# Layer 0's expert results: gathered and summed in a stage of their own, or inside layer 1's first projection sweep

## The reference

```
proj = modulate(rms_norm(x)) @ w_in          # queries, keys, values of three attention branches
x    = x + mod[2] * merge_branches(...)      # this is "x1" in the kernel
h2   = modulate(rms_norm(x))
f    = hier_moe(h2)                          # top-2 of 32 SwiGLU experts: f = w0 * ye[row0] + w1 * ye[row1]
x    = x + mod[5] * f                        # "x2", the input of the next layer
```

## Time and profile before

| | us |
|---|---|
| median of 3 runs | 5008.48 |
| the profiled execution's own time | 5003.68 |
| its span | 5002.1 |
| PE busy | 4544.4 (91%) |
| DVE busy | 3310.6 (66%) |
| ACT busy | 2464.5 (49%) |
| POOL busy | 1192.3 (24%) |
| layer 0's jobs, about | 1927 to 2584 |
| layer 0's combine and change of stage, about | 2584 to 2637 |
| layer 1's jobs, about | 4244 to 4957 |
| layer 1's combine, about | 4957 to 5002 |

### The profile page before, as it was taken

The page is one execution under the profiler, slowest core; times in us unless marked ns, Lnnn a source line. Parts: engine busy times, 40 slices in busy tenths (PEclk is TensorE's granted clock), DMA queues, the critical chain, the costliest instruction groups (busy, mean ns, idle before and its releaser), DMA issues. The chain is left out here.

```text
span 5002.1 us, 75983 instructions
## 1 busy us (share of the span) xinstructions
PE 4544.4 (91%) x25973; PEld 3776.1 (75%) x25973; DVE 3310.6 (66%) x5272; ACT 2464.5 (49%) x3056; POOL 1192.3 (24%) x921
## 2 busy tenths in 40 slices
PE   6999998889999897999967999999999987999995
PEld 4887877777877875877745878888877866788774
DVE  6653667676776567777777626677756436877776
ACT  3223555564233315777743225655633222777774
POOL 3650004400000013333334620043000001333333
PEclk8999999999999998999988999999999998999998
DMA  5645234264554566999995635253556345999998
GB/s 188 206 120 122 65 87 104 100 185 139 209 201 168 207 210 262 397 397 397 397 357 169 199 113 117 63 124 97 136 191 217 113 167 174 388 397 397 397 397 330
DMA packets 581798, 1088.92 MB, mean 218 GB/s; under 512 B 111876, under 2 KB 265380, under 8 KB 578552
## 3 DMA queue, kind: packets, MB, share of 16 engines
q1 hardware_dynamic: 531952, 919.40, 54.8%
q0 software_dynamic: 36272, 119.42, 6.6%
q10 hardware_dynamic: 13400, 47.85, 2.4%
HBM read 903.12 MB, written 183.43 MB: 217 GB/s over the span
## 5 line engine op out<-in xcount | busy, mean ns | idle before, releaser
L1800 PE MATMUL merge_acc<-ahead_wide,merge_w_split 128*128 128x512 f32 (+1 forms) x2880 | 638.7, 377 | 20.5 <-DMA ahead_wide<-hT 14.9
L1800 PEld LDWEIGHTS merge_acc<-ahead_wide,merge_w_split 128*128 128x128 f32 x2880 | 505.4, 190 | 128.6 <-issue 18.7
L648 PE MATMUL project_proj_acc<-ahead_wide,project_hT 128*128 128x512 f32 x2280 | 562.1, 399 | 3.0 <-DVE ahead_wide L471 1.7
L2502 DVE TENSOR_TENSOR experts_w_gate<-experts_raw_gate,experts_w_gate 128x2048 fp32r<-128x2048 f32 x146 | 363.4, 2495 | 295.8 <-ACT experts_w_gate L2398 295.8
L648 PEld LDWEIGHTS project_proj_acc<-ahead_wide,project_hT 128*128 128x128 f32 x2280 | 426.1, 191 | 94.0 <-DVE project_hT L501 4.6
L2377 POOL TENSOR_TENSOR experts_w_down<-experts_raw_down,experts_w_down 128x2048 fp32r<-128x2048 f32 x73 | 355.9, 4876 | 512.5 <-ACT experts_w_down L2398 512.5
L2549 PE MATMUL experts_gate_acc<-experts_w_gate,experts_rowsT 128*128 128x512 f32 x1752 | 432.2, 403 | 13.2 <-DVE experts_rowsT L2507 6.9
L964 DVE TENSOR_REDUCE attend_stat<-attend_scores 128x1 f32<-128x1280 f32 (+2 forms) x288 | 305.7, 1061 | 205.9 <-PE attend_scores L865 202.2
L2563 PE MATMUL experts_result_acc<-experts_w_down,experts_hiddenT 128*128 128x512 f32 x1752 | 430.1, 401 | 12.2 <-DVE experts_w_down L2502 12.2
L2549 PE MATMUL experts_up_acc<-experts_w_up,experts_rowsT 128*128 128x512 f32 x1752 | 420.6, 395 | 0.0
L2549 PEld LDWEIGHTS experts_gate_acc<-experts_w_gate,experts_rowsT 128*128 128x128 f32 x1752 | 327.0, 190 | 101.5 <-issue 22.0
(11 more groups left out here) (257 smaller groups left out, 8298.5 us busy)
## 6 DMA issues: line engine op xcount, KB each, us to landing
experts_raw_gate<-in_w_exp_gate_dram SPq DMA_DIRECT2D x146, 1024.0 KB, 13.8
experts_raw_up<-in_w_exp_up_dram SPq DMA_DIRECT2D x146, 1024.0 KB, 12.8
experts_raw_down<-in_w_exp_down_dram SPq DMA_DIRECT2D x146, 1024.0 KB, 11.4
ahead_rows<-in_w_merge_dram SPq DMA_DIRECT2D x120, 768.0 KB, 6.4
merge_mod_w_ada<-in_w_ada_rows_dram POOLq DMA_DIRECT2D x80, 512.0 KB, 3.7
qk<-project_staged SPq DMA_DIRECT2D x74, 512.0 KB, 3.4
ye<-ahead_rows ACTq DMA_DIRECT2D x73, 512.0 KB, 6.3
attend_keys<-qk SPq DMA_DIRECT2D x96, 320.0 KB, 5.6
```

The lines of the kernel that those rows point to most:

```text
L648: m = pe.matmul(acc[g % 2][:, :], hT[:, a, q * KP + k, t * P:(t + 1) * P], w_split[n % SLOTS][:, c, k, :], start=(q == 0 and i == 0 and k ...
L1800: m = pe.matmul(acc[:, b, 0:w], w_split[b][:, a, k, :], hT[:, x, k, 0:w], start=(i == 0 and k == 0), stop=(i == 2 and k == KD - 1))
L2502: dve.tensor_tensor(w[n][:, 1, half, :], raw[n][:, half, :], w[n][:, 0, half, :].bitcast(F32), ALU.subtract).then_inc(w_lo[n].sem, 1)
```

## The change

1. In layer 0 there is no combine. The rows and weights that it used (`row_of`, `weight`) move into two small buffers that live through the whole kernel (`carried`), and the experts' stage returns after the jobs.
2. In both layers the job's result is multiplied by the gate row on its way out of PSUM. VectorE does it (`result`), after the lo of down's first half; ScalarE's copy is gone, and ScalarE only issues the store, for the job before. Where there are context tokens (layer 0), VectorE first picks the gate row per token: a compare on the token's number (GpSimd copies the numbers to `row_token`), a `scalar_tensor_tensor` of two gate rows into `y`, and then the product. The gate rows (1 MB) are loaded at the start of the jobs.
3. In layer 1's projection GpSimd gathers the two rows of each tile, two buffers each, which lie in split buffers that sweep 1's weights use later. VectorE adds both to the `x1` tile in place, with two `scalar_tensor_tensor` (`add_results`), ScalarE stores the latent tiles to `x2` (`store_x2`), and the norm's in-place scaling waits for that store. The splits of sweep 1's first two pieces move from steps 3 and 5 to 7 and 8.
4. Layer 1's combine has two `scalar_tensor_tensor` on VectorE per tile in place of ScalarE's product and VectorE's three operations.

```diff
 def project_heads(nc, io, scr, l, nq, st, inner, ident, hT, ahead, carried):
+    SUM = l > 0
+    result = [[w_split[4 + b][:, c, :, :].rearrange("p k n -> p (k n)").bitcast(F32) for b in range(2)] for c in range(2)]
+    split_at = (7, 8) if SUM else (3, 5)
...
 # SyncE
+                src = scr["x1"][t * P:(t + 1) * P, :] if SUM else stream_rows(io, scr, l, t)
+                sp.dma_start(xh[t % RING][:, :], src).then_inc(x_in[t % RING].sem, 16)
...
 # ScalarE
+            def store_x2(t):
+                act.wait_ge(x_ready.sem, x_ready.done(t))
+                act.dma_start(scr["x2"][t * P:(t + 1) * P, :], xh[t % RING][:, :]).then_inc(x2_out[t % 2].sem, 16)
...
+            if SUM:
+                store_x2(0)
             norm(0)
+            if SUM:
+                store_x2(1)
             norm(1)
...
                     if 0 <= g - 2 < n_heads:
                         heads_hi(g - 2)
+                    if SUM and p == 0 and s + 3 < NL:
+                        store_x2(s + 3)
...
 # VectorE
+            def add_results(t):
+                x, b = xh[t % RING], t % 2
+                dve.wait_ge(x_in[t % RING].sem, x_in[t % RING].done(t // RING))
+                dve.wait_ge(result_in[0][b].sem, result_in[0][b].done(t // 2))
+                dve.scalar_tensor_tensor(out=x[:, :], in0=result[0][b], scalar=carried.weight[:, 0, t:t + 1],
+                                         in1=x[:, :], op0=ALU.mult, op1=ALU.add).then_inc(added.sem, 1)
+                dve.wait_ge(result_in[1][b].sem, result_in[1][b].done(t // 2))
+                dve.wait_ge(added.sem, added.done(t))
+                dve.scalar_tensor_tensor(out=x[:, :], in0=result[1][b], scalar=carried.weight[:, 1, t:t + 1],
+                                         in1=x[:, :], op0=ALU.mult, op1=ALU.add).then_inc(x_ready.sem, 1)
...
                 dve.wait_ge(nrs.sem, nrs.done(t))
+                if SUM and t < NL:
+                    dve.wait_ge(x2_out[t % 2].sem, x2_out[t % 2].done(t // 2))
                 dve.scalar_tensor_tensor(out=x[:, :], in0=x[:, :], scalar=n_stat[:, b, 3:4],
...
                         if s + 1 < NT:
                             norm_lo(s + 1)
+                        if SUM and s + 3 < NT:
+                            add_results(s + 3)
...
 # GpSimd: gather(0), gather(1) first; gather(2), gather(3) after the first table; then ahead of each rotation
+                    if SUM and p == 0 and s + 4 < NT:
+                        gather(s + 4)
                     rotate(first[p] + s)
 
 def run_experts(...):
 # SyncE, after the first job's down weights
+            mod_rows(scr, l, 5, gate[:, :, :], sp).then_inc(gate_in.sem, 16)
...
 # ScalarE
-            def result(g):
-                act.wait_ge(dm.sem, dm.done(g))
-                if later(g, 1):
-                    act.wait_ge(y_out.sem, y_out.done(g - 1))
-                act.copy(y, acc_y[:, :]).then_inc(yd.sem, 1)
+            def store_result(g):
                 act.wait_ge(yd.sem, yd.done(g))
                 act.dma_start(scr["ye"][ds(g * P, P), :], y).then_inc(y_out.sem, 16)
...
-                if later(g, 1):
-                    result(g - 1)
+                if later(g, 2):
+                    store_result(g - 2)
                 act.wait_ge(ht.sem, ht.done(g))
...
 # VectorE
+            def result(g):
+                dve.wait_ge(dm.sem, dm.done(g))
+                if later(g, 1):
+                    dve.wait_ge(y_out.sem, y_out.done(g - 1))
+                row_gate = gate[:, 0, :]
+                if CONTEXT:
+                    dve.wait_ge(kind_read.sem, kind_read.done(g))
+                    take_waits(dve, gate_taken)
+                    dve.tensor_scalar(of_context[:, :], row_token[:, ds(g, 1)], float(NL * P), None, ALU.is_ge
+                                      ).then_inc(kind_known.sem, 1)
+                    dve.wait_ge(kind_known.sem, kind_known.done(g))
+                    dve.scalar_tensor_tensor(out=y, in0=gate[:, 1, :], scalar=of_context[:, 0:1],
+                                             in1=gate[:, 0, :], op0=ALU.mult, op1=ALU.add).then_inc(gate_picked.sem, 1)
+                    dve.wait_ge(gate_picked.sem, gate_picked.done(g))
+                    row_gate = y
+                dve.tensor_tensor(y, acc_y[:, :], row_gate, ALU.mult).then_inc(yd.sem, 1)
...
                 split(DOWN, g)
+                if later(g, 1):
+                    result(g - 1)
...
             result_rows()
             weights()
+            result(n_jobs - 1)
```

More of the change, by code:

```diff
@@ L261, in project_heads @@
     taken = st.event("pool_waits_taken")
+    added, x_ready = st.event("first_result_added"), st.event("x2_ready")
+    x2_out = [st.dma(f"x2_stored{b}") for b in range(2)]
+    result_in = [[st.pool_dma(f"result{c}_gathered{b}") for b in range(2)] for c in range(2)] if SUM else None
+    split_at = (7, 8) if SUM else (3, 5)
     tr, hh, hl, v_ev = (st.event("head_transposed"), st.event("head_hi"), st.event("head_lo"),
@@ L585, in rotate, with gather @@
                                    ).then_inc(tn.sem, 1)
+            def gather(t):
+                if t >= 2:
+                    pool.wait_ge(x_ready.sem, x_ready.done(t - 2))
+                take_waits(pool, taken)
+                for c in range(2):
+                    pool.indirect_dma_start(
+                        out=result[c][t % 2], out_offset=None, in_=scr["ye"],
+                        in_offset=bass.IndirectOffsetOnAxis(ap=carried.row_of[:, t, c:c + 1].bitcast(U32), axis=0)
+                    ).then_inc(result_in[c][t % 2].sem, 16)
             TABLE_AT = {(0, 3): 1, (0, 5): 2, (1, 2): 3, (2, 2): 4, (3, 2): 5}
+            if SUM:
+                gather(0)
+                gather(1)
             pool.wait_ge(tab_in.sem, tab_in.done(1))
@@ L2590, in _, with combine @@
             down(n_jobs - 1)
-def combine(nc, io, scr, l, nq, st, inner, row_of, weight, gate, gate_in, x1, x1_in, out):
+def combine(nc, io, scr, l, nq, st, inner, row_of, weight, x1, x1_in, out):
     y = [[st.sb(f"y{c}_{t}", [P, D], F32, inner) for t in range(nq)] for c in range(2)]
```

97 lines of the change are left out of this document (61 added, 36 removed).

## The result

The changed kernel takes 5074.82 us (median of 4 runs, 5069.22 to 5078.06), the kernel before 5007.78 beside it (5005.16 to 5009.58): ratio 1.0134, 95% interval 1.0122 to 1.0146, 1.3% slower. The forecast was 5074. The profiled execution took 5078.06 with a span of 5076.4, so 74.3 us are to be found between the two spans. That is 7 us more than the 67.0 between the two medians: this execution is the slowest of its four, and the profiled one of the kernel before (5003.68) is faster than any of its runs.

What follows compares the result with a forecast made beforehand. It took TensorE (99% busy, DMA also full) to bound the jobs, and DMA and VectorE the combine. 60 + 10 - 48 + 15 + 20 + 12 - 3.5 = +65.5 us gave 5069.2 profiled, 5074 median, range 5050 to 5098.

Steps and rivals of the forecast that it cites:

- a: Layer 0's jobs: period grows from 18.4 to 20.3 us as VectorE's down split is held beside GpSimd, +60 us.
- GpSimd lost only 0.9 us: Layer 0's jobs: GpSimd's down split, started beside VectorE's, took 5.72 instead of 4.80 us, so was barely held.
- the long state: Layer 0's jobs: the lost tie repeats itself, holding the period at 20.3 us for 32 of 34 periods.
- b: Last job of layer 0, from last gate product to last store issued: +10 us, bounds 5 and 13.
- c: Layer 0's combine goes, between last store issued and layer 1's first load: -48 us, bounds 46 and 49.
- d: Start of layer 1's projection: first transposes 9 us later, tile 2 adds 6, together +15 us, bounds 6 and 22.
- e: Sweep 0 of layer 1's projection, paced by VectorE, with result additions and waits for x2's store: +20 us, bounds 14 and 32.
- all of it visible: Sweep 0: seven steps' additions of 2 x 1.3 us on VectorE, 18.2 us, lengthen the sweep in full.
- f: Layer 1's jobs: the result's product can make VectorE's down split lose to GpSimd, +12 us, bounds 0 and 25.
- the first jobs run back to back and lose the race: Layer 1's first jobs: GpSimd starts before VectorE's down split; the reason for taking 12 of a possible 14 us.
- g: Layer 1's tail: VectorE's four steps per tile become two, transfers limit the gain, -3.5 us, bounds -8 and 0.
- the transfers' 30 us: Layer 1's tail: 16 gathers and 8 stores, 12.6 MB at 420 GB/s, need 30 of the 36.5 us.

Runs made afterwards that it cites:

- vector_all: Changed kernel, but VectorE splits both halves of the down weights in layer 0's jobs and GpSimd none: 5007.96 us, ratio 1.0010.
- no_pick: Changed kernel without the compare and scalar_tensor_tensor that choose layer 0's gate row, so context rows get a wrong gate: 5002.65 us, ratio 0.9999.
- reordered: Changed kernel with VectorE's gate-row choice behind the next gate split, its product ahead of the down split, and ScalarE's store behind the silu: 5028.11 us, ratio 1.0054.
- pool_copy: Changed kernel with GpSimd's tensor_tensor for the down weights replaced by a one-input tensor_copy, values wrong: 5000.63 us, ratio 0.9992.
- gate_late: Changed kernel with the 1 MB of gate rows loaded behind the first job's gate and up weights instead of ahead: 5068.34 us, ratio 1.0129.
- short_add: Changed kernel, but from tile 3 on the second result is added to only 128 of 1024 columns in layer 1's first sweep: 5063.18 us, ratio 1.0125.

## Why the prediction was right, and where it was off

**a, right (59.3 for 60).** The period is 20.21 for 20.3, from the fourth on (31 of 34; the first three are 19.4, 19.4 and 18.6). The marks came out: the down split held (6.38 us in the mean), the scalar_tensor_tensor short because it comes after GpSimd, TensorE released by VectorE's result. vector_all, no_pick and the periods of reordered show that the hold is the cause. **One step in it was wrong**: "GpSimd lost only 0.9 us". The 4.80 I compared with was itself held. In the kernel before GpSimd's instruction starts beside the end of VectorE's down split; in the early job of the earlier trace rows that split is:

```profile
1949.78 2.29 DVE L2502 TENSOR_TENSOR experts_w_down<-experts_raw_down,experts_w_down 128x2048 fp32r<-128x2048 f32 x1
```

With 1.24 us of it left (1952.07 - 1950.83) GpSimd took 5.72; with 0.33 left, 4.80 to 4.83 in most jobs; with 1.50 left, 5.99. All are 4.5 and what was left: each engine is held for all that remains of the other's instruction. (In no_pick, where in most jobs the split was already over, GpSimd takes 4.60 to 4.63.) The Trainium skill, page "SBUF — State Buffer", section "SBUF: two separate sides", says just this of the port pair that VectorE and GpSimd share: it is an exclusive lock, and the one who comes second blocks fully. The rows now agree for both sides. The page counts a VectorE instruction with two SBUF inputs only against a GpSimd instruction that reads SBUF; pool_copy agrees that one such input is enough on GpSimd's side. The slip made no difference to the sum, since in the long state GpSimd always comes first, and the two periods of reordered in which it came last are 20.3 as well.

**b, right (11.6 for 10)**; the choice of the gate row was held 4 us in the last job as well (5.33), and no_pick gave it back. The 1.6 over the forecast are mostly in the product of the job before: it took 7.41 us behind TensorE's wait, where the forecast has about 6.

**c, right (48.1 for 48).** The combine's stage is gone with all but one landing and the change of stage.

**d and e, right as a sum, with the parts off.** They are +10.1 for 9 to the first transposes, then +29.8 for 26, and +26.7 to +29.8 over the six kernels with that code. Of the 29.8, 12.6 lie between tile 0's and tile 2's transposes (9.4 to 12.6 over the six), where the forecast has 6, and 17.1 behind them, where it has 20. What the sum left out at the start is the last of the four weight pieces: SP issues its load 7.9 us after the first transposes, before it was 4.1, and ScalarE can cast it 15.9 us after them instead of 8.0 (11.0 in vector_all, 11.8 in gate_late). Tile 2's additions are queued behind its split. The cast before and after:

```profile
2657.05 1.05 ACT L403 CAST ahead_wide<-ahead_rows 128x1024 fp32r<-128x1024 f32 x1 [3.12 <-DMA ahead_rows<-in_w_heads_dram]
```

```profile
2700.59 1.04 ACT L412 CAST ahead_wide<-ahead_rows 128x1024 fp32r<-128x1024 f32 x1 [11.06 <-DMA ahead_rows<-in_w_heads_dram]
```

In the steps the wait for the store and its meeting with GpSimd are 3.4 to 6.5, most likely 3.5 (forecast 5.7), and the additions are not "all of it visible": of 7.5 us in short_add 4.1 were. As an estimate from these runs, 55% of the 18.2 for the additions and 3.5 for the store make 13.5 of the 17.1, so a few microseconds of the steps have no cause shown.

**f, wrong in size (+2.6 for +12).** The step that failed is "the first jobs run back to back and lose the race". They did not: in layer 1 the result is one product out of PSUM, VectorE is at the down split in time, and the periods are 18.11 from the third on. The down splits of layer 1 take 2.28 us in the mean:

```profile
L2574 DVE TENSOR_TENSOR experts_w_down<-experts_raw_down,experts_w_down 128x2048 fp32r<-128x2048 f32 x36 | 82.1, 2281 | 2.3 <-ACT experts_w_down L2473 2.3
```

What layer 1 pays is the gate rows' load in its first two periods (20.3 and 20.5 for 17.6 and 18.1), which gate_late took back; the bound at which later periods turn from 18.1 to 18.5 is then met later, at the 16th period instead of the 9th.

**g, wrong in size (+0.1 for -3.5).** The last store comes 1.2 us later, as forecast, but from the first gather to the last addition the gain is 1.1 us (35.4 for 36.5), not 4.7. The term that failed is the transfers' 30 us: I had taken 420 GB/s for them from 10 us of layer 0's combine. (36.5 less 30 would also be 6.5; how 4.7 came of it the prediction doesn't say.) The windows of the two tails, before and after:

```profile
4961.50:4998.00 36.50, 0.00 (x0) 0.00 (x0) 29.24 (x24) 9.18 (x8) 15.44 (x16) 0.50 0.86 330
```

```profile
5037.00:5073.00 36.00, 0.00 (x0) 0.00 (x0) 20.56 (x16) 0.00 (x0) 17.98 (x16) 0.50 0.89 335
```

Over the whole window, the first landing included, the transfers run at 330 to 335 GB/s in both. Before, VectorE waited 9.5 us for the first gather and for none behind it; now, with 20.6 us of work instead of 29.2, it waits 18.4 us in all, 8.4 for the first. So the transfers set the tail, and nearly all of the work that was saved came back as waits.

f and g together were 6 us too high, the untouched stretches 9 us too low, and a to e 6 us too low: the sum forecast was 65.5, between the profiled executions it is 74.4 and between the medians 67.0. That the median was hit to 1 us is partly chance; the 60 and the -48 are not.

## What to carry to other kernels

Before work is moved onto VectorE, look for what stands beside the place: a VectorE instruction with two SBUF inputs that starts a moment after one of GpSimd's that reads SBUF costs its own length and GpSimd's (6.51 us for 2.29 here), so 2.7 us that fit a slack of 4.1 by size cost 1.8 us in each of 31 jobs. Then the cure can be to give VectorE more work and GpSimd none. And a stage that is removed brings only what its waits were worth: the hole before layer 1 became 36 us shorter, and the additions, the store and the gathers, moved into the next stage's first sweep, made that 30 us longer.

## What the runs showed of the hardware

GpSimd's own small work grows beside VectorE's split as well. In the long jobs the gather's issue (L2442) takes 2.61 us in the mean instead of 1.0, and the cast of one column (L2447) 1.35 instead of 0.21; from the changed kernel's timeline, beside VectorE's gate split of 2223.76 to 2228.24:

```profile
2224.18 2.74 POOL L2442 DMA_INDIRECT ahead_rows<-h,experts_index  x1 [4.62 <-DMA experts_index<-token_of]
...
2226.91 1.37 POOL L2447 CAST experts_row_token<-experts_index 128x1 int32 x1
```

The cast ends at 2228.28, with the split. It cost nothing that a run here shows: the period is set by the down split and the result.

Small operations of VectorE are held just so. In no_pick a `tensor_tensor` on 128x32 elements (L2546) that starts at 2578.62, beside GpSimd's last half of 2577.22 to 2581.97, takes 3.40 us; in the changed kernel, with GpSimd idle, it takes 0.18.
